# Half of a level-by-level matrix inverse is made by transposes instead of matmuls, and a head pass is reordered on three engines

## What is computed

```python
kk = jnp.einsum('nbhid,nbhjd->nbhij', kc, kc)
a_strict = jnp.where(strict, bc[..., :, None] * kk * jnp.exp(diff), 0.0)
lower_unit = a_strict + jnp.eye(GDN_CHUNK, dtype=a_strict.dtype)
rhs = jnp.concatenate([vc * bc[..., None], kc * (bc * jnp.exp(gcum))[..., None]], axis=-1)
sol = lax.linalg.triangular_solve(lower_unit, rhs, left_side=True, lower=True, unit_diagonal=True)
```

## Time and profile before

| | us |
|---|---|
| median of 3 runs (1722.97 to 1723.35) | 1723.27 |
| the profiled execution | 1713.79 |
| its span, first to last instruction | 1712.0 |
| PE busy in the span | 1654.2 (97%) |
| DVE busy | 1154.5 (67%) |
| ACT busy | 729.9 (43%) |
| POOL busy | 116.2 (7%) |

### The profile page before, as it was taken

The page is one execution under the profiler, slowest core; times in us unless marked ns, Lnnn a source line. Parts: engine busy times, 40 slices in busy tenths (PEclk is TensorE's granted clock), DMA queues, the critical chain, the costliest instruction groups (busy, mean ns, idle before and its releaser), DMA issues.

```text
span 1712.0 us, 27574 instructions
## 1 busy us (share of the span) xinstructions
PE 1654.2 (97%) x10466; PEld 1440.8 (84%) x10466; DVE 1154.5 (67%) x1690; ACT 729.9 (43%) x1177; POOL 116.2 (7%) x215
## 2 busy tenths in 40 slices
PE   5997999999999999999999899999999999999997
PEld 1255999898999999999999788888888888888886
DVE  3635788788888888677777755555555555655655
ACT  1445353534445353532435644444444444343341
POOL 1001110101111110000010000000000000111110
PEclk9999999999999999999999999999999999999999
DMA  9995343443434343422698144445544446877873
GB/s 374 398 366 210 111 149 125 149 149 102 166 108 165 123 148 125 172 99 77 255 328 324 69 178 180 188 195 196 196 189 180 180 187 225 282 247 251 287 246 107
DMA packets 83234, 334.10 MB, mean 195 GB/s; under 512 B 8059, under 2 KB 24502, under 8 KB 56706
## 3 DMA queue, kind: packets, MB, share of 16 engines
q1 hardware_dynamic: 62304, 257.97, 40.6%
q0 software_dynamic: 19600, 68.25, 12.2%
q10 hardware_dynamic: 1234, 6.57, 1.0%
HBM read 328.56 MB, written 4.19 MB: 194 GB/s over the span
## 4 chain that ended last, share of the span: by engine, by line
PE 87%; DMA 6%; DVE 4%; ACT 1%; issue 1%; DVEq 1%; POOL 0%; ACTq 0%; POOLq 0%
PE g L479 10%; PE o L479 9%; PE o L472 8%; PE o L474 8%; PE o L473 8%; PE g L480 5%; PE o L480 5%; DMA w_mod_tile_o<-in_w_mod_t 4%; PE g L563 3%; PE g L558 3%; PE o L486 2%; PE g L486 2%; PE g L488 2%; PE o L488 2%; PE g L487 2%; PE o L487 2%
## 5 line engine op out<-in xcount | busy, mean ns | idle before, releaser
L453 DVE TENSOR_TENSOR w_lo<-w_raw,w_hi 128x2048 fp32r<-128x2048 f32 x203 | 464.9, 2290 | 219.3 <-ACT w_hi L448 218.7
L448 ACT CAST w_hi<-w_raw 128x2048 fp32r<-128x2048 f32 x204 | 389.8, 1911 | 333.9 <-PE o L474 180.5
L472 PE MATMUL o<-h_hi,w_hi 128*128 128x256 f32 (+1 forms) x896 | 298.4, 333 | 0.8 <-DVE w_lo L453 0.8
L474 PE MATMUL o<-h_hi,w_lo 128*128 128x256 f32 (+1 forms) x896 | 282.0, 315 | 0.0
L473 PE MATMUL o<-h_lo,w_hi 128*128 128x256 f32 (+1 forms) x896 | 281.5, 314 | 0.0
L479 PE MATMUL g<-h_hi_lo,w_hi 128*128 128x512 f32 x704 | 245.0, 394 | 0.0
L479 PE MATMUL o<-h_hi_lo,w_hi 128*128 128x512 f32 x688 | 240.5, 394 | 2.1 <-DVE h_hi_lo L1942 2.1
L480 PE MATMUL g<-h_hi_lo,w_lo 128*128 128x256 f32 x704 | 195.0, 277 | 0.0
L480 PE MATMUL o<-h_hi_lo,w_lo 128*128 128x256 f32 x688 | 190.6, 277 | 0.0
L474 PEld LDWEIGHTS o<-h_hi,w_lo 128*128 128x128 f32 x896 | 170.8, 191 | 11.3
L472 PEld LDWEIGHTS o<-h_hi,w_hi 128*128 128x128 f32 x896 | 171.4, 191 | 10.2 <-issue 3.3
(11 more groups left out here) (376 smaller groups left out, 2852.3 us busy)
## 6 DMA issues: line engine op xcount, KB each, us to landing
w_raw<-in_w_ff_t SPq DMA_DIRECT2D x88, 1024.0 KB, 6.3
w_raw<-in_w_heads_t SPq DMA_DIRECT2D x56, 1024.0 KB, 4.9
w_mod_raw<-in_w_mod_t SPq DMA_DIRECT2D x32, 1024.0 KB, 10.5
w_raw<-in_w_down_t SPq DMA_DIRECT2D x32, 1024.0 KB, 6.8
w_mod_piece_h<-in_w_mod_t POOLq DMA_DIRECT2D x112, 256.0 KB, 3.9
w_raw<-in_w_out_t SPq DMA_DIRECT2D x16, 1024.0 KB, 8.5
w_mod_tile_o<-in_w_mod_t POOLq DMA_DIRECT2D x16, 1024.0 KB, 9.7
w_mod_piece_d<-in_w_mod_t POOLq DMA_DIRECT2D x64, 256.0 KB, 5.9
```

Source lines behind the costliest of these rows:

```text
L448: e.copy(whi[p.split[j]][:], raw[p.raw[j]][:]).then_inc(hi_ready, 1)
L453: e.tensor_tensor(wlo[p.split[j]][:], raw[p.raw[j]][:], whi[p.split[j]][:].bitcast(F32), ALU.subtract).then_inc(lo_ready, 1)
L472: e.matmul(o, a, xh, start=first, stop=False)
L474: return e.matmul(o, b, xh, start=False, stop=last)
```

## The change

- The running natural inverse in Z and its matmuls (`U1` to `U5`, and half of `u`) are gone. Only X is kept. `u` is four transposes into X.
- From level 2 on, a new ACT step `X` copies the whole of X from PSUM into `bD`, after DVE's `DT` of the level. A new PE step `DN` transposes those four squares into Z, and DVE masks Z into `bD` as before.
- In level 1, D is the mask of `bY` in SBUF (new step `D1`).
- `qe`, which read Z, is now waited for in `DN2`.
- The lists of the head pass and of the tail pass are in a new order on all three engines.

```diff
-        STEPS = {"ip": ["tok", "dec", "kT", "qT", "kk", "u"] + [x for l in LV for x in (f"Y{l}", f"UT{l}", f"U{l}") if x != "U6"],
-                 "ia": ["lf", "vt", "sq", "e2", "e1", "qn", "kT", "qT", "qe"] + [f"Y{l}" for l in LV],
-                 "iv": ["hv", "nr", "kt", "A", "U0", "ag"] + [x for l in LV for x in (f"M{l}", f"DT{l}", f"D{l}")] + ["Z"],
+        STEPS = {"ip": ["tok", "dec", "kT", "qT", "kk", "u"] + [x for l in LV for x in (f"DN{l}", f"Y{l}", f"UT{l}") if x != "DN1"],
+                 "ia": ["lf", "vt", "sq", "e2", "e1", "qn", "kT", "qT", "qe"] + [x for l in LV for x in (f"X{l}", f"Y{l}") if x != "X1"],
+                 "iv": ["hv", "nr", "kt", "A", "U0", "D1", "ag"] + [x for l in LV for x in (f"M{l}", f"DT{l}", f"D{l}") if x != "D1"] + ["Z"],
...
             elif step == "u":
                 w_iv(pe, h, "U0")
-                w_ia(pe, h, "qe")
                 for c in range(NCHUNK):
-                    pe.matmul(X[:, at_chunk(c)], bY[:, c], IDN, start=(c == 0), stop=True, skip_group_check=True)
-                for c in range(NCHUNK):
-                    last = pe.matmul(Z[:, at_chunk(c)], IDN, bY[:, c], start=(c == 0), stop=True, skip_group_check=True)
+                    last = pe.matmul(X[:, at_chunk(c)], bY[:, c], IDN, start=(c == 0), stop=True, is_transpose=True,
+                                     skip_group_check=True)
...
+            elif step[:2] == "DN":
+                w_ia(pe, h, f"X{n}")
+                if n == 2:
+                    w_ia(pe, h, "qe")
+                for c in range(NCHUNK):
+                    last = pe.transpose(Z[:, at_chunk(c)], bD[:, c], IDN)
+            else:
                 w_ia(pe, h, f"Y{n}")
                 w_iv(pe, h, f"D{n}")
                 for c in range(NCHUNK):
                     last = pe.matmul(X[:, at_chunk(c)], bD[:, c], bY[:, c], start=False, stop=True, skip_group_check=True)
-            else:
-                for c in range(NCHUNK):
-                    last = pe.matmul(Z[:, at_chunk(c)], bY[:, c], bD[:, c], start=False, stop=True, skip_group_check=True)
...
+            pr(0); pr(1); pr(2); pr(3); scan("z0"); uh(); inv("tok"); scan("s0"); pr(4); scan("k1"); inv("dec"); pr(5)
+            scan("z1"); pr(6); scan("s1"); pr(7); inv("kT"); inv("qT"); scan("k2"); inv("kk"); pr(8); pr(9); scan("z2")
+            pr(10); inv("u"); scan("s2"); pr(11); pr(12); scan("k3"); inv("Y1"); pr(13); inv("UT1"); scan("o2"); scan("z3")
+            pr(14); inv("DN2"); scan("o3"); inv("Y2"); pr(15); inv("UT2"); pr(16); pr(17); pr(18); inv("DN3"); inv("Y3")
+            pr(19); inv("UT3"); pr(20); pr(21); scan("tr"); inv("DN4"); inv("Y4"); pr(22); pr(23); inv("UT4"); pr(24); pr(25)
+            pr(26); inv("DN5"); inv("Y5"); pr(27); pr(28); pr(29); inv("UT5"); pr(30); pr(31); inv("DN6"); inv("Y6"); mod()
+            inv("UT6")
...
+            inv("UT1"); pr(13); inv("DN2"); inv("Y2"); scan("tr"); pr(14); inv("UT2"); pr(15); inv("DN3"); inv("Y3")
+            pr(16); inv("UT3"); pr(17); inv("DN4"); inv("Y4"); pr(18); inv("UT4"); pr(19); inv("DN5"); inv("Y5"); pr(20)
+            inv("UT5"); pr(21); inv("DN6"); inv("Y6"); uh2(); pr(22); inv("UT6"); pr(23); hu(0); scan2("z0"); pr(24); scan2("s0"); hu(1)
...
+            elif step[0] == "Y":
                 w_ip(act, h, step)
                 last = act.activation(bY[:], chunks(Y), ACT.Copy, scale=-1.0)
+            else:
+                w_iv(act, h, "DT" + step[1])
+                last = act.copy(bD[:], chunks(X))
...
+                rp(); inv("lf"); scan("vs0"); inv("vt"); inv("sq"); inv("be"); inv("e2"); scan("vs1"); inv("e1"); inv("qn")
+                inv("kT"); inv("qT"); mc(); uhc(); inv("qe"); scan("vs2"); re(0); ev(0); inv("Y1"); inv("X2"); scan("vn3")
+                scan("os"); inv("Y2"); re(1); inv("X3"); inv("Y3"); ev(1); th_(0); re(2); inv("X4"); inv("Y4"); ev(2); re(3)
+                ev(3); th_(1); inv("X5"); ev(4); inv("Y5"); re(4); inv("X6"); th_(2); tz(); ev(5); inv("Y6")
...
+            elif step == "D1":
+                v.drain()
+                w_ip(v, h, "dec")
+                last = v.tensor_tensor(bD[:], bY[:], mid(lev[:, 7]), mulv)
...
-            elif step[0] == "D":
-                w_ip(v, h, f"U{n - 1}" if n > 1 else "u")
+            elif step[0] == "D" and n > 1:
+                w_ip(v, h, f"DN{n}")
...
+                inv("hv"); pc(0, 1); scan("v0"); pc(1, 2); rp(); pc(2, 3); cc(); pc(3, 4); scan("S0"); scan("v1"); pc(4, 5)
+                scan("w1"); inv("nr"); pc(5, 6); inv("kt"); pc(6, 7); scan("S1"); inv("bb"); scan("v2"); pc(7, 8); scan("w2")
+                pc(8, 9); inv("A"); pc(9, 10); inv("U0"); pc(10, 11); scan("v3"); inv("D1"); inv("ag"); inv("M1"); scan("S2")
+                inv("DT1"); re(0); scan("w3"); pc(11, 12); inv("M2"); inv("DT2"); cv(0); inv("D2"); scan("nb"); inv("M3")
+                inv("DT3"); re(1); inv("D3"); at_(); pc(12, 13); inv("M4"); inv("DT4"); cv(1); inv("D4"); scan("mix"); re(2)
+                inv("M5"); sm(0); inv("DT5"); cv(2); re(3); pc(13, 14); inv("D5"); inv("M6"); pc(14, 15); cv(4); pc(15, 16)
+                inv("DT6"); sm(1); re(4); inv("D6"); cv(5); sm(2); mod(); inv("Z"); zm()
...
+                inv("M1"); inv("DT1"); scan("nb"); inv("M2"); inv("DT2"); inv("D2"); cv(1); inv("M3"); re(2)
                 inv("DT3"); inv("D3"); scan("mix"); inv("M4"); cv(2); inv("DT4"); inv("D4"); re(3); zm(); inv("M5")
-                inv("DT5"); cv(3); inv("D5"); inv("M6"); at_(); inv("DT6"); inv("D6"); re(4); inv("Z"); scan2("v0"); hp(0)
+                inv("DT5"); inv("D5"); cv(3); inv("M6"); at_(); inv("DT6"); inv("D6"); re(4); inv("Z"); scan2("v0"); hp(0)
```

More of the change, by code:

```diff
@@ L781, in tail_pe @@
             inv("kk"); scan("o2"); scan("z3"); pr(8); pr(9); inv("u"); scan("o3"); pr(10); inv("Y1"); pr(11); pr(12)
-            inv("UT1"); pr(13); inv("U1"); inv("Y2"); scan("tr"); pr(14); inv("UT2"); pr(15); inv("U2"); inv("Y3"); pr(16)
-            inv("UT3"); inv("U3"); pr(17); inv("Y4"); pr(18); inv("UT4"); pr(19); inv("U4"); inv("Y5"); pr(20); inv("UT5")
-            inv("U5"); inv("Y6"); pr(21); inv("UT6"); uh2(); pr(22); hu(0); scan2("z0"); pr(23); scan2("s0"); hu(1); pr(24)
+            inv("UT1"); pr(13); inv("DN2"); inv("Y2"); scan("tr"); pr(14); inv("UT2"); pr(15); inv("DN3"); inv("Y3")
+            pr(16); inv("UT3"); pr(17); inv("DN4"); inv("Y4"); pr(18); inv("UT4"); pr(19); inv("DN5"); inv("Y5"); pr(20)
+            inv("UT5"); pr(21); inv("DN6"); inv("Y6"); uh2(); pr(22); inv("UT6"); pr(23); hu(0); scan2("z0"); pr(24); scan2("s0"); hu(1)
             scan2("k1"); hu(2); scan2("z1"); pr(25); scan2("s1"); pr(26); hb(0); pr(27); scan2("k2"); pr(28); hu(3); pr(29)
@@ L1805, in mod @@
                     modulation(v, g + 5, 1, g + 1, F[1])
-                inv("hv"); pc(0, 1); scan("v0"); pc(1, 3); cc(); pc(3, 4); scan("v1"); scan("S0"); pc(4, 5); scan("w1")
-                inv("nr"); scan("S1"); inv("kt"); inv("bb"); scan("v2"); scan("w2"); rp(); pc(5, 7); inv("A"); inv("U0")
-                scan("S2"); inv("ag"); scan("v3"); scan("w3"); pc(7, 10); inv("M1"); inv("DT1"); inv("D1"); scan("nb")
-                inv("M2"); inv("DT2"); inv("D2"); cv(0); inv("M3"); inv("DT3"); inv("D3"); re(0); pc(10, 13); inv("M4")
-                inv("DT4"); re(1); inv("D4"); inv("M5"); scan("mix"); cv(1); re(2); cv(2); sm(0); inv("DT5"); re(3)
-                inv("D5"); sm(1); at_(); pc(13, 16); inv("M6"); re(4); cv(4); inv("DT6"); sm(2); inv("D6"); cv(5); mod()
-                zm(); inv("Z")
+                inv("hv"); pc(0, 1); scan("v0"); pc(1, 2); rp(); pc(2, 3); cc(); pc(3, 4); scan("S0"); scan("v1"); pc(4, 5)
[5 more added lines that the diff above has]
+                inv("DT6"); sm(1); re(4); inv("D6"); cv(5); sm(2); mod(); inv("Z"); zm()
                 v.drain()
@@ L1875, in tail_dve @@
                 inv("hv"); scan("v0"); scan("S0"); scan("v1"); scan("w1"); scan("v2"); scan("S1"); scan("w2"); inv("nr")
-                scan("S2"); inv("kt"); inv("bb"); scan("v3"); scan("w3"); re(0); inv("A"); inv("U0"); re(1); inv("ag")
-                inv("M1"); inv("DT1"); inv("D1"); scan("nb"); inv("M2"); inv("DT2"); cv(1); inv("D2"); inv("M3"); re(2)
+                scan("S2"); inv("kt"); inv("bb"); scan("v3"); scan("w3"); re(0); inv("A"); inv("U0"); inv("D1"); re(1); inv("ag")
+                inv("M1"); inv("DT1"); scan("nb"); inv("M2"); inv("DT2"); inv("D2"); cv(1); inv("M3"); re(2)
                 inv("DT3"); inv("D3"); scan("mix"); inv("M4"); cv(2); inv("DT4"); inv("D4"); re(3); zm(); inv("M5")
-                inv("DT5"); cv(3); inv("D5"); inv("M6"); at_(); inv("DT6"); inv("D6"); re(4); inv("Z"); scan2("v0"); hp(0)
+                inv("DT5"); inv("D5"); cv(3); inv("M6"); at_(); inv("DT6"); inv("D6"); re(4); inv("Z"); scan2("v0"); hp(0)
                 scan2("v1"); scan2("S0"); cv(4); scan2("w1"); hp(1); scan2("v2"); re(5); scan2("S1"); cv(5); hp(2)
```

9 lines of the change are left out of this document (2 added, 7 removed).

## The result

The changed kernel takes 1695.0 us (median of 4 runs, 1687.7 to 1702.1), the kernel before 1723.1 beside it; the ratio is 0.9847, 95% interval 0.9812 to 0.9882. The prediction was 1693.5, with 1685 to 1706.

The account below looks back on a forecast made before the run. PE was taken to bound the kernel (87% of the span). 28.7 + 5.6 - 1.2 - 1.2 - 2.4 = 29.5 us took the profiled 1713.8 to 1684.3; the median forecast was 1693.5, range 1685 to 1706.

Parts of the forecast that it names:

- PE's records: In each head's inverse, one-record transposes replace two-record fp32 matmuls: 3.59 us saved a head, 28.7 us for eight.
- Waits that the order removes: In middle passes, PE's waits before `tok` (0.79 us) and at k1 (0.15) go: 0.94 a pass, 5.6 us in all.
- The wait at `kk`: In middle passes, a new PE wait for ACT's copy before `kk`: 0.2 us a pass, 1.2 us lost.
- Room in the loop of a level: In middle passes, the longer loop UT, DT, X, DN, D fits with about 1 us of room at its tightest link.
- DVE's waits: On DVE, 11.7 us of waits for U go; 14.6 were for modulation pieces; DVE, 89% busy, is late next.
- Pass 0: First head pass: 3.6 us gained less 1.2 of waits at `kk`, DN2 and UT2, so 2.4 us gained.
- The tail: Last head pass: 3.6 us gained less 2.4 of waits at DN, so 1.2 gained; later steps nothing, at most 2 more.
- The whole: Whole kernel: 29.5 us gained, the profiled execution 1713.8 to 1684.3 us, the median 1693.5.
- Late links: Rival, 12%: DVE makes DN or UT wait about 0.4 us a level in middle passes; 16 us lost, 1709.
- Two records a transpose: Rival, 2%: on PE, transposes cost two records each, as fp32 matmuls do; 1715 us.
- DVE sets the pass: Rival, 4%: DVE's 64.6 us of work plus 12.6 of waits keep the old 77.2 us pass; no gain, 1723.
- The clock falls: Rival, 3%: PE's clock drops around DN and Y in levels 3 to 6, 7.5 us lost a pass; 1754.

Follow-up runs that it names:

- run 1: The changed kernel with the old inverse put back (U kept, `u` twice) in the new lists of PE, ACT and DVE; 1718.5 us, ratio 0.9979.
- run 3: The changed kernel with DN and `u` as fp32 matmuls against the identity in place of transposes; 1709.3 us, ratio 0.994.
- run 5: The changed kernel with `kk` one piece later, U0 ahead of a modulation piece, and two tail splits moved on DVE; 1697.5 us, ratio 0.9839.
- Runs 7 and 8: The changed kernel with the mask DT computed twice (7) and three times (8) on DVE in every level; 1702.7 and 1747.1 us.
- the clean pair: Profiled executions of the kernel before (11) and of the changed kernel with two tail places moved (10), same feed-forward pace, no low clock; 1712.87 and 1682.21 us.
- run 4: The changed kernel once more, unchanged; 1691.8 us, ratio 0.9804.
- Run 9: The changed kernel with five moves in the tail only, on DVE, PE and ACT; 1688.7 us, ratio 0.9814.
- run 6: The changed kernel with DN3 done 24 times over in every pass, 96 transposes in a row; 1774.3 us.
- run 2: The changed kernel with the head pass lists in the old order, the tail keeping its new lists; 1735.6 us, ratio 1.0097.
- 11: The kernel before once more, unchanged, for a second profile; 1712.9 us.
- 10: The changed kernel with only `hv` and v_new ahead of DVE's first split and piece 1 ahead of PE's v_new matmuls, in the tail; single execution 1682.2 us.

## Why the prediction was right, point by point

- **PE's records** (28.7 us for eight heads; 3.59 a head). Right: 3.66 by runs 1 and after, the half of it 2.77 for 2.67 by run 3. 534 records a pass, as predicted; four transposes take 0.44.
- **Waits that the order removes** (0.94 a middle pass). Right in kind, 0.26 too small: run 1 shows 0.93 net of the new wait at `kk`, so 1.20 gross (0.1 less against the second profile of the kernel before, whose pass is 76.97). The wait at `tok` and 0.26 at k1 make up 1.05 of it; the rest is spread over steps too small to name. The 0.19 net that I had not counted and the 0.07 of the records, six times, are the 1.6 us by which the middle passes beat the forecast.
- **The wait at `kk`** (0.2 a pass). It is 0.27. Its mending was a new error (run 5): DVE's list behind `kk` has the same 0.2 us.
- **Room in the loop of a level** ("about 1 us"). Right: no wait at DN in any middle pass. The tightest links of pass 2 have 0.74 us (X4 ends that long before DN4, where the count had 1.5) and 0.76 (D6 ends before UT6). The old order shows what the room is for: without it six passes lose 7.5 us. Runs 7 and 8 were meant to measure this room and ran into DVE first.
- **DVE's waits.** The wait for pieces fell from 14.6 to 5.3, and the wait for U is gone, as said; that DT and D would wait for PE instead was not. "What is late next is DVE" was right, and nearer than it looked: 89% busy leaves 8 us a pass, but only 2.1 of them are waits.
- **Pass 0** (-2.4): -2.2 and, in the clean pair, -2.4. This one is read from the start of the program and scatters: the kernel after alone gives 231.03 us and, in run 4, 1.2 more.
- **The tail** (-1.2, and "nothing" for its later part, at most 2 more). This is the step that failed, by 2.2 us. The profiles of before, run 1 and after, all three with a low stretch of clock of the same length, part it: the new order, taken at nothing, costs 1.8, and the new inverse in it gains 0.9, against 1.2. The waits at DN are as foreseen. The list of waits shows 1.4 of them; the rest hides in the step itself, as the chain in order of time shows: each of the five DN takes 0.63 to 0.66 where four transposes take 0.44, 0.2 at each, together 2.45 against the 2.4 of the sum. But I had taken the later tail at nothing, and there the moved pieces of PE meet ACT's list: piece 24, the first of tile 6, writes the bank that the eviction of tile 4 frees. PE's list now has it ahead of s0, while on ACT that eviction still stands behind a wait for the last head's z0. The chain, kernel after:

```profile
707.18 0.65 PE g L562 x4
...
713.58 0.66 PE g L562 x4
...
737.38 0.23 PE g L598 x2
...
738.15 0.37 ACT pre_conv L1175
738.53 0.48 ACT hy_x L1176
739.00 0.14 issue
```

  PE stood still for 1.3 us there. Against 3.6 of saved records stand 2.45 + 1.3 + 0.24 at Y1 + 0.3 more at v_new = 4.3, a loss of 0.7; measured, with the same clock, 1.0 to 1.1, so 0.3 to 0.4 us stay open, 0.2 of them in the order. Run 9, which took the split waits, this one and most of the one at v_new away, gave 5.3 at the same clock.
- **The whole.** My sum was for the profiled execution, 1684.3, and it came out at 1695.5: 11.2 more, of which 9.3 are the feed-forward pace, 2.2 the tail, 1.0 the stage behind it (133.7 to 136.7 us over the profiles), 0.2 pass 0, less 1.6 in the middle passes. The median fits (1693.5 against 1695.0) because I carried over, unexplained, the 9.5 us by which the shown runs of before lay above their profile; that is the size of the slow pace, so the sum and the result stand on the same pace there, by inference. That the median came so close is luck to this extent: nothing in the working says which pace an execution has.
- **The rivals.** Late links: not in the middle passes, 1.4 us in the tail (the bound for a wait of 0.2 to 0.5 us at each of 40 DN is 8 to 20 us, not 8 to 18). Two records a transpose: out (run 3). DVE sets the pass: not in this kernel, whose PE works 72.47 of 72.48 us, but it is the next limit, 2.1 us of waits away, and it does so in runs 7 and 8. The clock falls: out, by the 1.00 in every middle pass and by run 6; the longest run of transposes in the new order is twelve, `uh` and `tok`, and not the ten of the prediction.

## What to carry to other kernels

When an engine's records are replaced by cheaper ones that depend on two other engines, count the loop from result to result and put that much foreign work of the bounding engine between: here the same change was a gain of 28 us with it and a loss of 13 without (run 2). The spare time of the next engine is its waits for others, not all that its busy share leaves: here 2.1 us of 8. Where a list is reordered, count the places behind it too, above all those in which another engine's wait stands ahead of an eviction; that is where the forecast failed. And measure between markers in the program (one step per pass) rather than by the whole time: stages that no edit touched moved here by 9 us from one execution to the next.

## What the runs showed of the hardware

- The feed-forward stage, PE busy throughout with the clock at 1.00, ran at one of two paces in the 13 profiles, 0.345 or 0.352 us for a pair of matmuls (391 to 394 and 399 ns for the larger one), the same through one execution: 9.3 us of 489.
- Behind the wait of about 3 us in the tail PE ran at the 1.2 GHz level for some 3 to 6 us (granted clock 0.50 to 0.57) in most profiles, and at 1.00 at once in runs 4 and 11, with the same wait. Behind 1.3 us (runs 9 and 10) it stayed at 1.00. Between two profiles of one kernel it costs 1.0 to 1.1 us. In the middle passes of all runs, where PE's waits were at most 1.4 us, the clock stayed at 1.00.
- An fp32 transpose of 128x128 is one record, 0.11 us apart in a row, an fp32 product with the identity two; 96 transposes in a row keep the 2.4 GHz level.
